# Query tiles between the units of one attention, expert steps in three phases in the other, and unread products in TensorE's waits

## The chip, the cores and the metric

The kernel runs on one core of one Trainium2 chip. The metric is device time in microseconds (us) of one execution; the median of three is used. The engines are TensorE (PE, with its weight loads PEld), VectorE (DVE), ScalarE (ACT), GpSimd (POOL) and SyncE (SP). They run side by side, each through its own list of instructions in order, and meet at semaphores.

## What is computed

One step of a two-layer encoder on 576 tokens of width 1024 (512 of a prompt, 64 of a running stream). Layer 0 mixes tokens with a chunked gMLP; then shared keys and values are made; layer 1 mixes tokens with sliding-window attention. Behind each mixer stands a PEER block, in which every token picks 16 of 16,384 one-neuron experts in each of 8 heads:

```python
q = (xb @ w_q).reshape(blk, PEER_HEADS, 2, D_HALF)
sc = jnp.einsum('thpd,hpnd->thpn', q, sub_keys)
...
act = jax.nn.gelu(jnp.einsum('thkd,td->thk', exp_u[idx], xb))
w = gate * act
return jnp.einsum('thk,thkd->td', w, exp_v[idx])
```

Attention: 16 heads of 64, 4 key heads, a window of three chunks of 64, a bias by distance, and a sink column in the softmax.

## The kernel before

The tokens are split. The "d" (dense) group is 256 of the prompt's tokens (chunks c = 0 and 1, of 128), the "g" (gathered) group is the other 320 (c = 2, 3 and 4, the last of 64). In a PEER block, the d tokens meet all experts: for each of 64 expert pairs TensorE computes `expert_scores` (tile U), ScalarE takes the gelu, VectorE multiplies by a gate matrix (`build`, `one_hot`, `gate_product`), and TensorE adds `expert_sums` (tile V). The g tokens have their chosen experts fetched by indirect DMA: 320 steps a layer, and each step fetches one row of u and v for 128 tokens (128 x 2048 numbers of 4 bytes, 1.05 MB) into one of six slots of gata and gatb. On VectorE a step is a dot product (`dot_x`, L1865) and a weighted add to acc (`axpy`, L1873); between the two ScalarE makes the weight (`weight`, L1243 and L1245: a gelu and a scaling). Those of acc follow each other.

Some of the 320 steps are done early, at named places of other stages. The table `AT` lists the places and how many steps stand at each, `EARLY` is their sum (57 in layer 0, 62 in layer 1), and `step0` spreads the rest over the 64 pairs: 4.5 for each of the first 48, and what is left over the last 16. So a step that is added to `AT` leaves the last 16 pairs of its layer.

The order on every engine is written by hand. A dense product for g tokens is a "tile" of 24 matmuls (L569 to L571: weights and inputs split into a high and a low part, made by ScalarE and GpSimd), and one for d tokens a tile of 8 (L585, 16 rows in the trace). PSUM has eight banks; `plan` counts for each bank how often it is filled (semaphores `full`) and released (`free`), and a product waits until the bank's last reader has released it.

Attention of a group walks over units (j, c), j one of 8 pairs of heads, c one of the group's chunks: 24 units in the g group, 16 in the d group. TensorE's loop runs, for iteration n, the scores of unit n (L937), the transposes of its probabilities three units late (`att_turn`, L954, `LAG` = 3) and the output product four units late (`att_out`, L979). VectorE adds the bias and takes the maximum (`att_max`, L1985 and L1991) and the reciprocal (`att_norm`, L1998); ScalarE does the exponentials (L1363) and copies the transposes to pT (`att_copy`) and the output out of its bank (`att_evac`). In the g group the bank of an output is released by VectorE (`att_low`, L2008), five units late, behind `att_max` and `att_norm` of its iteration. `out_place` names the bank: two in turn for g, one for d. For d tokens the query tiles stand between the units (`Q_AT`); for g tokens all eight stand ahead.

## Time and profile before

| | us |
|---|---|
| median of three executions | 3116.64 (3114.83 to 3118.16) |
| the profiled execution | 3122.2 |
| its span on the core | 3120.4 |

| engine | busy, us | share of the span |
|---|---|---|
| TensorE | 2931.9 | 94% |
| VectorE | 2438.8 | 78% |
| GpSimd | 1011.7 | 32% |
| ScalarE | 797.7 | 26% |

DMA moved 1042.99 MB at a mean of 334 GB/s. The busy share is an average over stages whose limits differ; the rows further down show single stages. The granted clock is 1.00 where TensorE runs at 2.4 GHz and 0.50 where it runs at 1.2 GHz.

### The profile page before, as it was taken

Reading aid. Unit: us, or ns where it says so; the run is one execution under the profiler, and the core shown is the slowest. Engines: PE = TensorE matmul, PEld = TensorE weight load, DVE = VectorE, ACT = ScalarE, POOL = GpSimd, SP = SyncE. Lnnn points to the kernel's source line nnn. Section 1 sums busy time; section 2 is a strip of 40 time slices with the busy share of each in tenths; the row PEclk is TensorE's granted clock in tenths of the full one; section 3 lists DMA queues with packets and bytes.
Section 4 is the critical chain, followed back from the end, with each engine's and each line's share of the span. In section 5 each row is a group of like instructions: output and inputs, shape, how many; then the busy total and the mean of one; then the engine's idle time right before and its main releaser. Section 6 shows DMA issues by size and latency. Waiting matters only on the chain. (4 is left out here: it accounts for less than half of the span.)

```text
span 3120.4 us, 46622 instructions
## 1 busy us (share of the span) xinstructions
PE 2931.9 (94%) x17374; PEld 2572.0 (82%) x17374; DVE 2438.8 (78%) x5309; ACT 797.7 (26%) x2330; POOL 1011.7 (32%) x837
## 2 busy tenths in 40 slices
PE   8899899999999999987898979989999999999977
PEld 7898789888888888876768857879888888888865
DVE  3387899888888888877444777998888888888877
ACT  5432222212211212211453262222212112111212
POOL 5532222322333332333554311222323333333331
PEclk9999999999999999998859989989999999999999
DMA  5327789999999999999403358778999999999996
GB/s 185 116 97 293 305 327 357 398 421 422 421 422 419 420 411 420 414 418 417 150 28 107 121 211 318 275 289 312 419 422 421 422 422 420 415 420 414 413 421 267
DMA packets 159966, 1042.99 MB, mean 334 GB/s; under 512 B 18480, under 2 KB 23920, under 8 KB 44096
## 3 DMA queue, kind: packets, MB, share of 16 engines
q0 software_dynamic: 92160, 671.13, 52.6%
q1 hardware_dynamic: 64224, 357.99, 29.3%
q10 hardware_dynamic: 3424, 11.96, 1.0%
q8 instruction: 75, 1.23, 0.2%
q14 instruction: 83, 0.68, 0.1%
HBM read 1033.28 MB, written 7.86 MB: 334 GB/s over the span
## 5 line engine op out<-in xcount | busy, mean ns | idle before, releaser
L822 PE MATMUL bank<-a,V 128*128 128x256 f32 x4096 | 931.7, 387 | 56.0 <-DVE a L1856 37.6
L809 PE MATMUL bank<-xd,U 128*128 128x256 f32 x4096 | 937.6, 388 | 2.6 <-DMA U<-uvd 2.6
L822 PEld LDWEIGHTS bank<-a,V 128*128 128x128 f32 x4096 | 794.6, 195 | 176.4 <-issue 41.1
L1472 POOL DMA_INDIRECT gata<-uvg,idxg x428 | 511.9, 1196 | 1184.8 <-DVE acc L1873 1148.9
L809 PEld LDWEIGHTS bank<-xd,U 128*128 128x128 f32 x4096 | 788.3, 195 | 110.6 <-DMA U<-uvd 3.6
L1865 DVE CUSTOM_DVE_ANT_0 gata<-gata,xrow 128x1024 f32<-128x1024 f32 x428 | 522.1, 1220 | 229.7 <-DMA gata<-uvg,idxg 225.2
L1243 ACT ACTIVATE act<-dot 128x1 f32<-128x1 f32 x640 | 129.5, 202 | 1669.9 <-DVE dot L1865 1668.0
L1873 DVE SCALAR_TENSOR_TENSOR acc<-gata,wgt,acc 128x1024 f32<-128x1024 f32 x428 | 547.5, 1279 | 5.8 <-ACT wgt L1245 5.6
L1472 POOL DMA_INDIRECT gatb<-uvg,idxg x212 | 235.3, 1110 | 599.0 <-DVE acc L1873 589.2
L1865 DVE CUSTOM_DVE_ANT_0 gatb<-gatb,xrow 128x1024 f32<-128x1024 f32 x212 | 258.8, 1221 | 103.5 <-DMA gatb<-uvg,idxg 101.4
L796 PEld LDWEIGHTS bank<-B,oneA 128*128 128x128 f16 x4096 | 279.1, 150 | 29.4 <-issue 14.1
L796 PE MATMUL bank<-B,oneA 128*128 128x32 f16 x4096 | 283.3, 246 | 13.2 <-DVE B L1845 6.5
L1873 DVE SCALAR_TENSOR_TENSOR acc<-gatb,wgt,acc 128x1024 f32<-128x1024 f32 x212 | 271.3, 1280 | 1.3 <-ACT wgt L1245 1.3
L585 PE MATMUL bank<-xd,raw 128*128 128x256 f32 x896 | 214.6, 396 | 7.2 <-DVE xd L1574 7.2
L585 PEld LDWEIGHTS bank<-xd,raw 128*128 128x128 f32 x896 | 174.9, 199 | 34.0 <-issue 9.4
L569 PE MATMUL bank<-xh,wh 128*128 128x320 f32 x544 | 179.1, 329 | 21.1 <-POOL xl L455 19.5
L1245 ACT ACTIVATE wgt<-act,gateg 128x1 f32<-128x1 f32 x640 | 188.8, 295 | 20.8
L570 PE MATMUL bank<-xl,wh 128*128 128x320 f32 x544 | 170.9, 314 | 0.0
L571 PE MATMUL bank<-xh,wl 128*128 128x320 f32 x544 | 170.8, 314 | 0.0
L1839 DVE TENSOR_TENSOR oneA<-iotaA,i 128x1024 f16<-128x1024 f16 x256 | 170.3, 704 | 0.0
L1507 POOL TENSOR_TENSOR wl<-raw,wh 128x1024 fp32r<-128x1024 f32 x48 | 115.4, 2406 | 106.8 <-ACT wh L1043 106.7
L569 PEld LDWEIGHTS bank<-xh,wh 128*128 128x128 f32 x544 | 105.0, 193 | 30.6 <-issue 29.1
(210 smaller groups left out, 2586.3 us busy)
## 6 DMA issues: line engine op xcount, KB each, us to landing
U<-uvd SPq DMA_DIRECT2D x128, 1024.0 KB
V<-uvd SPq DMA_DIRECT2D x128, 1024.0 KB
raw<-lin SPq DMA_DIRECT2D x152, 512.0 KB
gata<-uvg,idxg POOLq DMA_INDIRECT x428
hsp<-h ACTq DMA_DIRECT2D x2, 2304.0 KB, 16.8
hx<-hsp SPq DMA_DIRECT2D x2, 2304.0 KB, 17.4
gatb<-uvg,idxg POOLq DMA_INDIRECT x212
sk_g<-skT ACTq DMA_DIRECT2D x2, 1024.0 KB, 4.8
```

The lines of the kernel that those rows point to most:

```text
L569: pe.matmul(out, whi, xhi[:, k, :], start=(k == 0), stop=False, skip_group_check=True)
L570: pe.matmul(out, whi, xlo[:, k, :], start=False, stop=False, skip_group_check=True)
L571: mm = pe.matmul(out, wlo, xhi[:, k, :], start=False, stop=(k == DT - 1), skip_group_check=True)
L585: mm = pe.matmul(bank[b][:, 0:TD], raw[:, s, P * k:P * k + P], xo[k][:, :] if name == "od" else x[:, k, :], start=(k == 0), stop=(k == DT ...
L796: mm = pe.matmul(bank[2 + s][:, CHUNK * t:CHUNK * (t + 1)], oneA[:, s, t // TG, :, t % TG], B[:, s, part, :, t], start=(t == 0 and part == ...
L809: mm = pe.matmul(bank[s][:, TD * t:TD * t + TD], U[:, s, o:o + P], xd[:, k, :], start=(t == 0 and k == 0), stop=(k == DT - 1), skip_group_ ...
L822: mm = pe.matmul(bank[b][:, TD * (d % 2):TD * (d % 2) + TD], V[:, s, o:o + P], a[:, s, TD * k:TD * k + TD], start=(first and k == 0 and d ...
L1245: act.activation(wgt[:, k:k + 1], act8[:, k:k + 1], ACT.Copy, scale=gateg[:, s:s + 1])\
L1472: pool.indirect_dma_start(row(l, s), None, uvg[l], bass.IndirectOffsetOnAxis(idxg[:, s:s + 1], 0)).then_inc(g_in[s % SLOTS], 16)
L1839: ins = dve.tensor_tensor(oneA[:, s, u], iotaA[:, :, :], i1[:, None, t + TG * u:t + TG * u + TG].broadcast_to([P, P, TG]), ALU.is_equal)
L1865: dve.tensor_tensor_reduce(u, u, xrow[:, min(s // P, 2), :], 1.0, 0.0, ALU.mult, ALU.add, dot[:, s % 8:s % 8 + 1]).then_inc(dot_done, 1)
L1873: dve.scalar_tensor_tensor(out=acc[:, n, :], in0=row(l, s)[:, D:RD], scalar=wgt[:, s % 8:s % 8 + 1], in1=acc[:, n, :], op0=ALU.mult, op1=A ...
```

## The change

Seven things are done together.

1. In the g attention only two of the eight query tiles stay ahead; the other six (24 matmuls each) stand between the units, in iterations 2, 5, ... 17, and write bank 5. The outputs, which used banks 4 and 5 in turn, all use bank 4. ScalarE's and GpSimd's work on the weights of these tiles, and of the first four of the next product, moves in between too.
2. In the d attention a group of three steps no longer stands in one iteration. The dots stand in iteration n (n = 2, 6, 10, 14), the weights in n + 1, two of the sums in n + 2, the third ahead of the next group's dots.
3. Three more steps stand behind the d attention (`"end"`) and one more in layer 0 (`"two"`).
4. The search of the best experts of chunk 3 in layer 1 (`find_best`) moves from behind the d attention to ahead of it.
5. One of the two query tiles ahead of the d attention moves ahead of `second_rank(1, 0)`.
6. In layer 0 the second chunk's exponential, `second_rank` and `gathered_index` stand one tile earlier.
7. `unused` multiplies a tile of ones by itself, and nothing reads the product: 8 and 20 times at the start, 20 behind `gmlp_g`, 24 at the end of layer 0's experts, 20 behind the g attention's output product.

```diff
 SLOTS = 6
+ATT_DOTS = (2, 6, 10, 14)
...
 AT = (
-    [("mid1", 3), ("two", 1), *[(f"add{m}", 1 + (m in (0, 2, 4))) for m in range(7)], ("mid2", 4),
+    [("mid1", 3), ("two", 2), *[(f"add{m}", 1 + (m in (0, 2, 4))) for m in range(7)], ("mid2", 4),
...
      ("sel3", 3), ("sel4", 3), *[(f"hot{m}", 1 + (m % 4 == 0 or m in (6, 10, 14))) for m in range(LEAD)]],
-    [*[(f"att{n}", 3) for n in (3, 7, 11, 16)], *[(f"add{m}", 1) for m in range(7)], ("mid1", 4),
+    [*[(f"att{n}", 3) for n in ATT_DOTS], ("end", 3), *[(f"add{m}", 1) for m in range(7)], ("mid1", 4),
...
     lin("kvg")
-    lin("qg")
+    seg("qg", b2=1, b3=1)
     seg("vng", b6=2, b7=1)
-    seg("attg", **{f"b{b}": 12 for b in range(8)})
+    seg("qxg", b5=6)
+    seg("attg", b0=12, b1=12, b2=12, b3=12, b4=24, b6=12, b7=12)
...
     seg("qd", b2=1, b3=1)
-    seg("qx", b5=6)
+    seg("qxd", b5=6)
...
-        Q_AT = {2 * m - 3: m for m in range(2, DT)}
+        Q_AT = {"g": {3 * m - 4: m for m in range(2, DT)}, "d": {2 * m - 3: m for m in range(2, DT)}}
...
-            return (4 + n % 2, n // 2) if grp == "g" else (4, n)
+            return 4, n
...
                 xhi, xlo = (oh, ol) if name == "outg" else (xh2, xl2) if name == "qg" else (xh, xl)
-                out = bank[s][:, 0:TG_]
+                b, n = tile_bank(name, m)
+                out = bank[b][:, 0:TG_]
                 pe.wait_ge(lo_done[s], LO[name] + m // 4 + 1)
-                pe.wait_ge(free[s], BASE[name][s] + m // 4)
+                pe.wait_ge(free[b], n)
...
                         norm_sum("n1d", m - 1)
+                    if m == 8:
+                        second_rank(0, 1)
                     if m == 9:
-                        second_rank(0, 1)
-                    if m == 10:
...
                     norm_sums("n5d")
+                else:
+                    pe.wait_ge(free[2], BASE["bld0"][2] + NBLD // 2)
+                    unused(2, 24)
...
+            def unused(b, n):
...
+                for _ in range(n):
+                    pe.matmul(bank[b][:, 0:P], ones[:, :], ones[:, :], start=True, stop=True, skip_group_check=True)
...
                 pe.nop().then_inc(full[b], 1)
+            pe.wait_ge(ones_done, 1)
+            unused(5, 8)
             pe.wait_ge(consts_in, 16 * 2)
-            pe.wait_ge(ones_done, 1)
             norm_sums("n0g")
+            unused(5, 20)
             gmlp_g()
+            unused(5, 20)
...
                 tile("kvg", m, "kv")
-            for m in range(DT):
+            for m in range(2):
...
                         wk = keys(c)[1][m]
-                        mm = pe.matmul(bank[ob][64 * e:64 * e + 64, 0:w], vv, pT[0:wk, n % 2, 2 * e + m, 0:w],
+                        mm = pe.matmul(bank[ob][64 * e:64 * e + 64, 0:w], vv, pT[0:wk, 2 * e + m, 0:w],
...
-                for m in range(DT - 4, DT) if grp == "g" else range(2):
-                    pe.wait_ge(*tile_out(f"q{grp}", m))
+                name, per = f"q{grp}", len(CHUNKS[grp])
+                for m in range(2):
+                    pe.wait_ge(*tile_out(name, m))
...
                     if n < len(UNITS[grp]):
-                        if grp == "d" and n % 2 == 0:
-                            pe.wait_ge(*tile_out("qd", n // 2))
+                        if n % per == 0:
+                            pe.wait_ge(*tile_out(name, n // per))
...
                         att_out(grp, n - LAG - 1)
-                    if grp == "d" and n in Q_AT:
-                        tile_d("qd", Q_AT[n], xd)
-                for n in range(len(UNITS[grp]) - 2, len(UNITS[grp])):
-                    ob, on = out_place(grp, n)
-                    pe.wait_ge(free[ob], BASE[f"att{grp}"][ob] + on + 1)
+                    if n in Q_AT[grp]:
+                        tile(name, Q_AT[grp][n], None, xd)
+                pe.wait_ge(free[4], BASE[f"att{grp}"][4] + len(UNITS[grp]))
...
             added("og", "n4g", None, None, None)
+            unused(5, 20)
...
                 tile_d("kvd", m, xkv, (nv_done, DT * APPLY["kvd"]))
+            tile_d("qd", 0, xd, (nv_done, DT * APPLY["mix1d"]))
...
             gathered_index(1, 0, (1,))
-            for m in range(2):
-                tile_d("qd", m, xd, (nv_done, DT * APPLY["mix1d"]))
+            tile_d("qd", 1, xd)
...
                         gate_exp(0, 0)
-                    if m == 8:
+                    if m == 7:
...
                     if grp == "d":
-                        weights_at(1, f"att{n}")
-                        if n in Q_AT:
-                            query("d", Q_AT[n])
+                        weights_at(1, f"att{n - 1}")
+                    if n in Q_AT[grp]:
+                        query(grp, Q_AT[grp][n])
+                        if grp == "g":
+                            ahead("qg", Q_AT[grp][n])
+                if grp == "d":
+                    weights_at(1, "end")
...
                         low_part(pool, PARTS["mix1"], dt, xl_done)
-            later_lows("qg")
-            first_lows("og")
+            later_lows("qg", (4, 5))
...
                                        ALU.mult).then_inc(pn_done, 1)
+                m = Q_AT["g"].get(n, 0)
+                if 2 <= m < 4:
+                    later_lows("qg", (m + 4,))
+                elif m >= 4:
+                    first_lows("og", (m - 4,))
...
+                return take_best(l, i, find_best(l, i, step))
...
+            def find_best(l, i, step):
...
                 last.then_inc(top_step, 1)
-                step += 1
+                return step + 1
...
+            def take_best(l, i, step):
...
+                c = ORDER[i]
+                n = TCS[c]
...
                 dve.wait_ge(oh_done, n + 1)
-                dve.tensor_tensor(xl[:, j, span("g", c)], bank[4 + n % 2][:, 0:TCS[c]],
-                                  xh[:, j, span("g", c)].bitcast(F32), ALU.subtract).then_inc(free[4 + n % 2], 1)
+                b = out_place("g", n)[0]
+                dve.tensor_tensor(xl[:, j, span("g", c)], bank[b][:, 0:TCS[c]],
+                                  xh[:, j, span("g", c)].bitcast(F32), ALU.subtract).then_inc(free[b], 1)
...
                     if grp == "d":
-                        steps_at(1, f"att{n}")
+                        dots_at(n)
+                        sums_at(n - 2)
+                if grp == "d":
+                    steps_at(1, "end")
...
+            def dots_at(n):
...
+                for k, s in enumerate(early(1, f"att{n}")):
+                    if k == 0 and s > 0:
+                        axpy(1, s - 1)
+                    dot_x(1, s)
...
+            def sums_at(n):
...
+                for s in early(1, f"att{n}")[:-1]:
+                    if s == 0:
+                        dve.wait_ge(acc_zero, 2)
+                    axpy(1, s)
...
             step = choose(1, 0, step)
+            step = find_best(1, 1, step)
...
             normed("n4d", G_FFN1, "d")
-            step = choose(1, 1, step)
+            step = take_best(1, 1, step)
```

TensorE, gathered attention, before: the output product of a unit of chunk 3 in bank 4, then the next iteration, whose output (chunk 4) is in bank 5, then the scores of the next.

```order
L979 MATMUL bank4<-pT_g_113,vnat_118 64x128 x4
L937 MATMUL bank1<-kvs_117,qT_g_108 128x128
L937 MATMUL bank7<-kvs_117,qT_g_108 128x128
L954 MATMUL bank2<-ident_77,S_g_110 128x128 x2
L979 MATMUL bank5<-pT_g_113,cvs_116 64x64
L979 MATMUL bank5<-pT_g_113,vnat_118 64x64
L979 MATMUL bank5<-pT_g_113,cvs_116 64x64
L979 MATMUL bank5<-pT_g_113,vnat_118 64x64
L937 MATMUL bank0<-kvs_117,qT_g_108 128x256
L937 MATMUL bank6<-kvs_117,qT_g_108 128x256
L954 MATMUL bank3<-ident_77,S_g_110 128x128 x4
L979 MATMUL bank4<-pT_g_113,vnat_118 64x128 x2
```

TensorE, the same place in the changed kernel: the transposes of a unit of chunk 4, the output product of chunk 3, and the first rows of a query tile (24 in all).

```order
L969 MATMUL bank2<-ident_77,S_g_110 128x64
L969 MATMUL bank2<-ident_77,S_g_110 64x64
L969 MATMUL bank2<-ident_77,S_g_110 128x64
L969 MATMUL bank2<-ident_77,S_g_110 64x64
L994 MATMUL bank4<-pT_g1_114,vnat_120 64x128 x4
L573 MATMUL bank5<-xh2_60,wh_55 128x320
L574 MATMUL bank5<-xl2_61,wh_55 128x320
L575 MATMUL bank5<-xh2_60,wl_56 128x320
```

The tile now stands between the output and the next scores, in bank 5, and every output product names bank 4.

VectorE, dense attention, before: the iteration that holds the first group of three steps (ISA is the dot product and its read-out).

```order
L1991 TENSOR_REDUCE nm<-S_d_112 128x2
L1998 RECIPROCAL rin<-den 128x2
L2002 TENSOR_SCALAR S_d_111<-S_d_111,rin 128x256
L1865 ISA gata,dot<-gata,xrow 128x1024
L1865 ISA dot 128x1
L1865 ISA gata,dot<-gata,xrow 128x1024
L1865 ISA dot 128x1
L1873 SCALAR_TENSOR_TENSOR acc<-gata,wgt,acc 128x1024
L1865 ISA gata,dot<-gata,xrow 128x1024
L1865 ISA dot 128x1
L1873 SCALAR_TENSOR_TENSOR acc<-gata,wgt,acc 128x1024
L1979 COPY S_d_111<-snk 128x2
```

VectorE, dense attention, in the changed kernel: the iteration with the first three dots, and the start of the next.

```order
L2023 TENSOR_REDUCE nm<-S_d_111 128x2
L2030 RECIPROCAL rin<-den 128x2
L2034 TENSOR_SCALAR S_d_112<-S_d_112,rin 128x256
L1897 ISA gata,dot<-gata,xrow 128x1024
L1897 ISA dot 128x1
L1897 ISA gata,dot<-gata,xrow 128x1024
L1897 ISA dot 128x1
L1897 ISA gata,dot<-gata,xrow 128x1024
L1897 ISA dot 128x1
L2011 COPY S_d_112<-snk 128x2
L2017 SCALAR_TENSOR_TENSOR S_d_112<-dst,bank 128x256 x2
L2023 TENSOR_REDUCE nm<-S_d_112 128x2
```

And its next iteration but one, with two of the sums.

```order
L2011 COPY S_d_111<-snk 128x2
L2017 SCALAR_TENSOR_TENSOR S_d_111<-dst,bank 128x256 x2
L2023 TENSOR_REDUCE nm<-S_d_111 128x2
L2030 RECIPROCAL rin<-den 128x2
L2034 TENSOR_SCALAR S_d_112<-S_d_112,rin 128x256
L1905 SCALAR_TENSOR_TENSOR acc<-gata,wgt,acc 128x1024 x2
L2011 COPY S_d_112<-snk 128x2
```

The dots and the sums, which alternated in one iteration, now stand two iterations apart.

## Rows read from the trace of the kernel before

**Rows 1.** The page's 40 slices: the DMA share in tenths.

```profile
DMA  5327789999999999999403358778999999999996
```

**Rows 2.** The page's groups: one line of expert products.

```profile
L809 PE MATMUL bank<-xd,U 128*128 128x256 f32 x4096 | 937.6, 388 | 2.6 <-DMA U<-uvd 2.6
```

**Rows 3.** Busy time by stretch, with TensorE's granted clock and DMA share.

```profile
core 0: us, PE busy (x) PEld busy (x) DVE busy (x) ACT busy (x) POOL busy (x), PEclk, DMA share, GB/s
135.30:140.60 5.30, 5.08 (x24) 4.86 (x25) 4.05 (x8) 2.16 (x5) 2.83 (x3) 0.73 0.30 94
1521.60:1565.20 43.60, 43.49 (x290) 42.54 (x291) 14.87 (x21) 20.48 (x36) 33.42 (x18) 1.00 0.40 132
1566.50:1638.60 72.10, 65.93 (x368) 42.48 (x369) 37.99 (x145) 38.30 (x154) 38.81 (x49) 0.54 0.06 17
1766.80:1775.10 8.30, 7.10 (x33) 5.90 (x32) 8.23 (x74) 2.05 (x3) 6.47 (x13) 1.00 0.41 132
1790.90:1875.60 84.70, 60.76 (x384) 44.43 (x385) 57.62 (x130) 50.46 (x149) 15.19 (x11) 0.84 0.58 225
3000.00:3074.00 74.00, 58.85 (x248) 49.21 (x246) 52.69 (x68) 9.96 (x40) 23.66 (x19) 0.94 1.01 419
```

**Rows 4.** Timeline, TensorE: one triple of the gathered attention; then one row of the dense.

```profile
1599.75 1.22 PE L937 MATMUL bank<-kvs,qT_g 64*128 64x256 f32 x4
1601.95 0.70 PE L979 MATMUL bank<-pT_g,vnat 128*64 128x128 f32 x4
1602.58 0.70 PE L937 MATMUL bank<-ck,qT_g 64*64 64x128 f32 x4
1604.20 1.13 PE L979 MATMUL bank<-pT_g,vnat 128*64 128x128 f32 x8
1605.26 0.80 PE L937 MATMUL bank<-kvs,qT_g 64*128 64x128 f32 x4
1606.60 0.48 PE L979 MATMUL bank<-pT_g,cvs 128*64 128x64 f32 x2
...
1608.22 0.80 PE L937 MATMUL bank<-kvs,qT_g 64*128 64x256 f32 x2
...
1818.50 0.72 PE L937 MATMUL bank<-kvs,qT_d 64*128 64x128 f32 x8
```

**Rows 5.** Timeline, VectorE, in the same two places.

```profile
1601.01 0.75 DVE L1985 SCALAR_TENSOR_TENSOR S_g<-dst,bank 128x256 f32<-128x256 f32 x2 [2.07 <-PE bank L937]
1602.53 0.20 DVE L2008 TENSOR_TENSOR xl<-bank,xh 128x64 fp32r<-128x64 f32 x1
1604.76 0.26 DVE L2008 TENSOR_TENSOR xl<-bank,xh 128x128 fp32r<-128x128 f32 x1
1607.07 0.26 DVE L2008 TENSOR_TENSOR xl<-bank,xh 128x128 fp32r<-128x128 f32 x1
...
1819.24 0.75 DVE L1985 SCALAR_TENSOR_TENSOR S_d<-dst,bank 128x256 f32<-128x256 f32 x2 [7.82 <-PE bank L937]
```

**Rows 6.** Who waited, TensorE, dense attention (1790.9 to 1875.6).

```profile
PE bank L979 <- ACT xo L1399: 23.5, 8, 7.3
```

**Rows 7.** Groups of lines, VectorE, dense attention.

```profile
L1873 DVE SCALAR_TENSOR_TENSOR acc<-gata,wgt,acc 128x1024 f32<-128x1024 f32 x8 | 10.3, 1282 | 1.9 <-ACT wgt L1245 1.9
L1865 DVE CUSTOM_DVE_ANT_0 gata<-gata,xrow 128x1024 f32<-128x1024 f32 x8 | 9.7, 1218 | 0.0
```

**Rows 8.** Timeline, ScalarE, one table load in the dense attention.

```profile
1801.91 1.28 ACT L1243 ACT_TABLE_LOAD   x1
```

**Rows 9.** Who waited: TensorE at 127 to 142.

```profile
PE bank L569 <- POOL xl L455: 6.3, 1, 6.3
```

**Rows 10.** Who waited: TensorE at 255 to 275.

```profile
PE bank L627 <- ACT vn_d L1089: 1.4, 1, 1.4
```

**Rows 11.** Who waited: VectorE at 1783 to 1792.

```profile
DVE S_d L1985 <- PE bank L937: 8.1, 1, 8.1
```

**Rows 12.** Who waited: TensorE at 1774 to 1778.

```profile
PE bank L744 <- issue: 3.1, 1, 3.1
```

More of the change, by code:

```diff
@@ L254, in program @@
               "d1": at_("S_d1", 155712, [P, 2, 2, 2 * P + 1], F32)}
-        pT_ = {"g": at_("pT_g", 36928, [P, 2, 4, P], F32), "d": at_("pT_d", 87040, [P, 2, 4, P], F32)}
+        pT_ = {"g": [at_(f"pT_g{s}", 36928 + 2048 * s, [P, 4, P], F32) for s in range(2)],
+               "d": [at_(f"pT_d{s}", o, [P, 4, P], F32) for s, o in enumerate((153600, 209504))]}
         ck = at_("ck", 41024, [P, 2, P], F32)
@@ L403, in tile_bank @@
         def tile_bank(name, m):
-            if name != "qd":
+            if name not in ("qg", "qd"):
                 return m % 4, BASE[name][m % 4] + m // 4
             if m < 2:
-                return 2 + m, BASE["qd"][2 + m]
-            return 5, BASE["qx"][5] + m - 2
+                return 2 + m, BASE[name][2 + m]
+            return 5, BASE["qx" + name[1]][5] + m - 2
         def tile_done(name, m):
@@ L573, in tile_g @@
                         mid()
-                mm.then_inc(full[s], 1)
+                mm.then_inc(full[b], 1)
             def tile_d(name, m, x, ready=None, mid=None):
@@ L960, in att_out @@
                 j, c = UNITS[grp][n]
-                w, pT = TCS[c], pT_[grp]
+                w, pT = TCS[c], pT_[grp][n % 2]
                 base = BASE[f"att{grp}"]
@@ L1345, in query @@
                                scale=DH ** -0.5).then_inc(free[b], 1)
-            for m in range(DT):
+            for m in range(2):
                 query("g", m)
@@ L1375, in att_copy @@
                 j, c = UNITS[grp][n]
-                w, wks, pT = TCS[c], keys(c)[1], pT_[grp]
+                w, wks, pT = TCS[c], keys(c)[1], pT_[grp][n % 2]
                 base = BASE[f"att{grp}"]
@@ L1382, in att_copy @@
                 if wks == [P, P]:
-                    act.activation(pT[:, n % 2, :, :], bank[2 + n % 2][:, :].rearrange("p (a q) -> p a q", a=4),
+                    act.activation(pT[:, :, :], bank[2 + n % 2][:, :].rearrange("p (a q) -> p a q", a=4),
                                    ACT.Copy).then_inc(free[2 + n % 2], 1)
@@ L1386, in att_copy @@
                 src = bank[2 + n % 2][:, :].rearrange("p (e m q) -> p e m q", e=2, m=2)
-                dstp = pT[:, n % 2, :, :].rearrange("p (e m) q -> p e m q", e=2)
+                dstp = pT[:, :, :].rearrange("p (e m) q -> p e m q", e=2)
                 for m, wk in enumerate(wks):
@@ L1500, in first_lows, with later_lows @@
                                        ALU.subtract).then_inc(lo_done[m], 1)
-            def later_lows(name):
-                for m in range(4, count(name)):
+            def later_lows(name, tiles=None):
+                for m in tiles or range(4, count(name)):
                     s = m % 4
```

## The prediction

> **What bounds the kernel now.** I read the page's slices first: the DMA share is near full from slice 7 to 19 and from 29 on, and low between, where layer 1 starts [rows 1]. So the expert phases run at the pace of their bytes (3000 to 3074: DMA 1.01 at 419 GB/s [rows 3]), and the rest at the pace of TensorE or of a chain through it. The busy time by stretch then shows three kinds of stretch outside the expert phases [rows 3]. Twelve tiles of the g kind take 43.6 us, full, at clock 1.00: 3.6 us a tile. The gathered attention takes 72.1 us with TensorE busy for 65.9, but at clock 0.54: the engine is full and slow. The dense attention takes 84.7 us with TensorE busy for 60.8 at clock 0.84, and its waits are one line: 23.5 us in 8 waits for ScalarE's copy of an output [rows 6]. A change outside the expert phases moves the end by what it saves there; one inside them counts by its bytes.
>
> **The change, part by part.** The sum is made against the profiled execution's own 3122.2 us, which lies 5.6 above the median of the runs; the difference is then taken from the median.
>
> *Four steps done earlier.* A step fetches 1.05 MB, and leaves the last 16 pairs of its layer, where DMA is full: 1.05 MB at 419 GB/s is 2.5 us [rows 3]. Four give -10.0. Where they go, VectorE has room: a step costs it a dot and a sum, 2.5 us [rows 7], and the stretch behind the dense attention has TensorE alone at work. Bounds: -10 (all bytes count), 0 (something else sets the tail's pace, for there TensorE is busy 58.9 of 74 us).
>
> *The gathered attention.* The stage and its six tiles now cost 72.1 + 6 x 3.6 = 93.7 us. Take one triple of units, from the scores of chunk 3 at 1599.75 to the next at 1608.22: 8.47 us, TensorE never waiting [rows 4]. With one bank, the output product in an iteration must wait until `att_low` of the same iteration has released it, and that stands on VectorE behind the maximum, which waits for this iteration's scores. The rows give how long that is, from the start of the scores to the end of L2008: 1602.73 - 1599.75 = 2.98, 1605.02 - 1602.58 = 2.44, 1607.33 - 1605.26 = 2.07 [rows 4, 5]. Behind each comes the output product, 0.63, 1.06 and 1.62 by the starts of the rows [rows 4]. With 0.1 a piece for the hand-over (an estimate) the triple is 11.1 us at 1.2 GHz. At 2.4 GHz the scores reach VectorE after 0.74 instead of 1.26 [rows 4, 5]; I take 0.52, 0.35 and 0.30 off the three and 0.59 (0.74/1.26) of the outputs: 6.3 + 2.0 + 0.3 = 8.6. So the second bank's loss costs what the clock can give back. Six triples carry a tile: 12.2 at 2.4 GHz; at 1.2 GHz 11.1 + 7.2 = 18.3. The first triple has no outputs to wait for, -2.7. All at 2.4: 6 x 12.2 + 2 x 8.6 - 2.7 = 87.7, or -6. All at 1.2: 129, or +36. Which? Before, the clock fell in the attention, where the matmuls are narrow, and came back with tiles; the dense attention, which has tiles between its units and waits too, was granted 0.84, that is a third of its time at 1.2 GHz [rows 3]. With the same third here, about a quarter of the work is at 1.2: 6 x 13.7 + 2 x 9.2 - 2.7 = 98. I take 97, **+3**, for the tiles take a little less of the cycle than there. GpSimd's weight parts hide behind the tile, and nobody on the chain waits for them.
>
> *The dense attention.* Before, a group's three dots and sums take VectorE about 7.3 us (3 x 1.15 + 3 x 1.2 and a short wait [rows 7]), and ScalarE's table load of 1.28 [rows 8], weights and second load lie beside them. In the changed order VectorE's block is 3 dots and a sum, 4.7 us, and ScalarE's block (two table loads, three weights, a query copy: 4.3 us) comes behind the next exponential, which waits for the maximum behind the dots. So the two no longer lie side by side: 9.0 instead of 7.3, +1.7 a group, and the two sums later hold the maximum up for 2.4, which TensorE's tile covers in part. Over four groups I take +8. The last group, formerly in the drain, is in the loop and cannot hide behind a tile. Against it: the query tile that moved ahead of `second_rank` fills a wait of 3.1 us [rows 12]. Net **+5**; bounds -15 (the phases hide the blocks, and most of the 23.5 goes) and +10.
>
> *`find_best`* takes 8.2 us of VectorE (the stretch 1766.8 to 1775.1, which is the same work on chunk 2 [rows 3]), and lands where VectorE waits 8.1 us for the first scores [rows 11]: 0. Where it left, VectorE gets no earlier, for its next product waits for TensorE's `second_rank`, whose place behind the third tile is the same: 0. Without that cover it would cost 8.
>
> *Layer 0's chunk one tile earlier*: VectorE reaches the copy that TensorE waits 1.4 us for sooner [rows 10]: **-1.4**, bounds 0 and -3. The extra step there fits in VectorE's slack.
>
> *The unread products.* One costs half of a 128 x 256 product, which is two records of 0.229 us [rows 2]: 0.23, and 20 cost 4.6 us. They stand in two waits of 6.3 us, behind `gmlp_g` [rows 9] and behind the g output product, where the kernel's wait is of the same kind, so they delay nothing. What they can give is the next tile's start: 5.3 us at clock 0.73 instead of 3.6 [rows 3], so 1.7 a place, 3.4 in all. I take three quarters, **-2.6**, since a wait of some 2 us is left. The Trainium skill (TensorE: Matmul & The Clock Gate, Part 1) says that the slow clock is the default and that activity lifts it; by that both places give their 1.7, and the sum would be 0.8 lower. At the start and at the end of layer 0's experts the wait left behind them is several us long: 0. Bounds -5 and, if they run at 1.2 GHz and outlast the wait (9.2 us against 6.3), +6.
>
> Sum: -10.0 + 3 + 5 - 1.4 - 2.6 = -6.0. From 3122.2 that is 3116.2 for such a profiled execution, and from the median 3116.6 it is **3110.6**. What a measurement of this kernel can tell from no change is about 0.2%, 6.2 us, so the forecast lies on the edge between "same" and "faster".
>
> **The rivals.**
>
> *The clock holds.* If the tiles keep 2.4 GHz through the gathered attention, the stage is 87.7 and the sum -15: **3102**. For it: tiles brought the clock back each time, and between two of them are only 8.6 us. Against it: the same narrow products ran at 0.54 with TensorE full.
>
> *The clock falls between the tiles* (the slower side). The waits for bank 4 leave TensorE idle for about 1.3 us in each unit, more than a third of the time between tiles, on top of narrow products. If each tile starts at 1.2 GHz and the attention behind it falls back soon, six tenths of the work is at 1.2: 6 x 15.9 + 2 x 10.1 - 2.7 = 113, or +19 instead of +3: **3127**. It decides from a stage of about 103 us on (no gain left), and is slower by over 0.2% from 109. The Trainium skill (same page, HAM oscillation) describes bursts between waits that each start cold; by that this rival is the likelier one, and here it would be a tile of over 5 us in each triple.
>
> *The three phases hide the blocks.* If dots, weights and sums each fit behind a unit and a tile, the 23.5 us shrink to 5 and the stage gives -15 to -20: **3090**. For it: a block alone is shorter than before. Against it: ScalarE's block now has no partner.
>
> *The early steps are worth nothing*, since VectorE or TensorE paces the tail: -10 falls away: **3120**. Against it: DMA at 1.01 in the very stretch.
>
> **How the numbers follow.** Forecast as it stands (3104 to 3117): 0.36, half of it over the edge. Clock holds: 0.20. Phases hide: 0.12. Clock falls: 0.18, nearly all slower by over 0.2%. Steps worth nothing: 0.14, a third of it slower in company of a dearer dense attention. Faster by over 0.2%: 0.18 + 0.20 + 0.12 = 0.50; slower: 0.18 + 0.05 = 0.23; same: 0.27. The range leaves out the deeper half of "phases hide" and the dearer part of "clock falls": 3093 to 3127.
>
> **What would show it.** Right: in the gathered attention a wait at the line of the output product for VectorE's line of `att_low` in nearly every unit, of 1 to 1.5 us; a granted clock near 0.85; the stage with its tiles 93 to 100 us. In the dense attention waits for ScalarE's copy of 25 to 35 us. The tile behind `gmlp_g` under 4 us. The last 16 pairs 7.5 us shorter in layer 1 and 2.5 in layer 0. Wrong: no waits for bank 4, or a clock of 0.6 there; a dense attention under 75 us; tails as long as before.

## The result, and the profile after

The changed kernel takes 3134.57 us (median of five, 3133.22 to 3138.15), the kernel before 3117.05 (five, 3114.83 to 3121.56). The ratio is 1.0054 with a 95% interval of 1.0042 to 1.0065: slower by 13 to 20 us, where 3110.6 was forecast with a range of 3093 to 3127. The profiled execution of the changed kernel has a span of 3132.8 against 3120.4, 12.4 us more. That is less than the 17.5 us between the medians, because the profiled execution of the kernel before (3122.2 us) lies 5 us above its median; the forecast's sum was made against that execution too, and gave -6.0 there.

Where the time went is read from TensorE's instructions, the same one in both traces. By how much it comes later than before:

| place | before | changed | later by |
|---|---|---|---|
| first product behind layer 0's experts (a shared-key tile) | 1521.6 | 1520.1 | -1.5 |
| end of the gathered attention's last output | 1638.0 | 1654.2 | 16.2 |
| first scores of the dense attention | 1790.9 | 1804.4 | 13.5 |
| end of its last output | 1875.2 | 1896.9 | 21.7 |
| first sums of pair 48, layer 1 | 2942.4 | 2962.2 | 19.7 |
| end of the last sums | 3095.0 | 3107.2 | 12.2 |

So the gathered attention and its tiles lost 17.7 us, the dense attention 8.2; the stretch between them gained 2.7, the work from there to pair 48 2.0 and the last 16 pairs 7.5. Busy time by stretch (columns as in rows 3), the kernel before: the gathered attention from its first scores to its last output, and the dense attention.

```profile
1567.00:1638.00 71.00, 65.93 (x368) 42.45 (x368) 37.51 (x143) 38.01 (x152) 38.45 (x49) 0.53 0.05 17
1790.90:1875.20 84.30, 60.75 (x384) 44.42 (x384) 57.62 (x130) 50.18 (x148) 15.19 (x11) 0.84 0.58 224
```

The changed kernel: the gathered attention with the six tiles in it, and the dense attention.

```profile
1544.40:1654.20 109.80, 83.60 (x512) 64.21 (x512) 40.47 (x143) 46.95 (x164) 52.30 (x55) 0.71 0.13 40
1804.40:1896.90 92.50, 61.86 (x384) 45.09 (x384) 63.67 (x156) 49.95 (x148) 18.41 (x14) 0.82 0.56 205
```

109.8 us stand against 92.6 of before (71.0 and six tiles of 3.6), at a clock of 0.71. Who waited, TensorE, in the gathered attention (1531 to 1652; the very last output, behind it, waits 0.8 us more):

```profile
PE bank L994 <- DVE xl L2041: 22.9, 21, 2.7
```

This is the wait that the forecast named: the output product for the release of bank 4 by `att_low`, 21 times, 1.1 us on average. In the dense attention the same view has, against 23.5 us in 8 waits [rows 6]:

```profile
PE bank L994 <- ACT xo L1414: 26.0, 11, 5.3
PE bank L994 <- ACT pT_d L1398: 2.5, 1, 2.5
```

And behind `gmlp_g`, where 6.3 us of wait stood [rows 9], the unread products leave:

```profile
PE bank L573 <- POOL xl L458: 1.8, 1, 1.8
```

The timeline of TensorE shows what follows the waits for bank 4: rows of a triple with its tile, then the start of the next tile.

```profile
1573.28 1.13 PE L994 MATMUL bank<-pT_g,vnat 128*64 128x128 f32 x8 [1.06 <-DVE xl L2041]
1574.34 0.64 PE L573 MATMUL bank<-xh,wh 128*128 128x320 f32 x1
1574.77 0.47 PE L574 MATMUL bank<-xl,wh 128*128 128x320 f32 x1
...
1578.23 0.31 PE L575 MATMUL bank<-xh,wl 128*128 128x320 f32 x1
...
1578.91 0.49 PE L952 MATMUL bank<-kvs,qT_g 64*128 64x128 f32 x4
...
1584.43 0.69 PE L994 MATMUL bank<-pT_g,vnat 128*64 128x128 f32 x4 [1.32 <-DVE xl L2041]
...
1587.64 1.13 PE L994 MATMUL bank<-pT_g,vnat 128*64 128x128 f32 x8 [1.06 <-DVE xl L2041]
1588.70 0.64 PE L573 MATMUL bank<-xh,wh 128*128 128x320 f32 x1
```

The tile begins with products of 0.64 and 0.47 us (1.2 GHz) and ends with products of 0.31 (2.4 GHz), so it takes 4.6 us; the six tiles take 3.78 (the first, at 2.4 GHz throughout), 5.23, 4.64, 5.86, 5.03 and 6.07. The clock comes back within each of the five others, holds for the narrow products behind it (scores in 0.49), and is down again when the next tile begins (the output ahead of it: 1.13).

### The profile page after: what moved, and what is told of

The parts are those of the page before. It is cut to its first block and busy times, and to the rows that moved or that the text cites. A ratio compares the mean times of both kernels' runs of the same rounds, so it can differ in the third digit from the quotient of the medians.

```text
span 3132.8 us, 46992 instructions
## 1 busy us (share of the span) xinstructions
PE 2942.9 (94%) x17558; PEld 2586.7 (83%) x17558; DVE 2443.1 (78%) x5309; ACT 798.2 (25%) x2330; POOL 1032.8 (33%) x837
## 5 line engine op out<-in xcount | busy, mean ns | idle before, releaser
L1491 POOL DMA_INDIRECT gatb<-uvg,idxg x212 | 257.2, 1213 | 522.3 <-DVE acc L1905 513.4
L573 PEld LDWEIGHTS bank<-xh,wh 128*128 128x128 f32 x544 | 107.0, 197 | 20.4 <-issue 16.6
```

Source lines behind the costliest of these rows:

```text
L573: pe.matmul(out, whi, xhi[:, k, :], start=(k == 0), stop=False, skip_group_check=True)
L1491: pool.indirect_dma_start(row(l, s), None, uvg[l], bass.IndirectOffsetOnAxis(idxg[:, s:s + 1], 0)).then_inc(g_in[s % SLOTS], 16)
```

## The experiments

"Theory" and "rival" in a quoted text are the outcomes named before the run. Every kernel was timed against the kernel before on the same chip, in four lots (the first four rows, the next four, four, three), in which the kernel before took 3117.9, 3118.5, 3120.5 and 3117.1. Across lots the ratios are the safer measure.

| kernel | time | ratio to before | 95% interval |
|---|---|---|---|
| e_gback | 3110.6 | 0.9977 | 0.9968 to 0.9986 |
| e_turnsg | 3111.9 | 0.9982 | 0.9973 to 0.9991 |
| e_nounused | 3133.1 | 1.0048 | 1.0034 to 1.0062 |
| e_onebank | 3135.9 | 1.0053 | 1.0039 to 1.0066 |
| e_steps | 3109.7 | 0.9966 | 0.9956 to 0.9977 |
| e_three | 3130.1 | 1.0033 | 1.0020 to 1.0046 |
| e_gdback | 3107.8 | 0.9967 | 0.9954 to 0.9980 |
| e_turnsgd | 3113.6 | 0.9986 | 0.9977 to 0.9996 |
| e_gfill | 3118.0 | 0.9995 | 0.9986 to 1.0004 |
| e_fill28 | 3136.1 | 1.0052 | 1.0038 to 1.0066 |
| e_nofind | 3104.7 | 0.9946 | 0.9932 to 0.9960 |
| e_best | 3109.2 | 0.9966 | 0.9954 to 0.9978 |
| e_bfill | 3112.6 | 0.9983 | 0.9974 to 0.9992 |
| e_turnsfill | 3097.2 | 0.9937 | 0.9923 to 0.9950 |
| e_backnofindfill | 3099.3 | 0.9946 | 0.9933 to 0.9960 |

### The gathered attention: one bank

**e_gback**: the changed kernel, its gathered attention as before.

```diff
-    seg("qg", b2=1, b3=1)
+    lin("qg")
...
-        Q_AT = {"g": {3 * m - 4: m for m in range(2, DT)}, "d": {2 * m - 3: m for m in range(2, DT)}}
+        Q_AT = {"g": {}, "d": {2 * m - 3: m for m in range(2, DT)}}
...
-            return 4, n
+            return (4 + n % 2, n // 2) if grp == "g" else (4, n)
...
```

> The changed kernel with the gathered attention as it was before (all eight query tiles ahead, outputs in banks 4 and 5 in turn), everything else of the change kept. Theory 1 (the 15 us that TensorE's instructions are late by the end of the gathered attention belong to this part, and nothing later gives them back): 3134.6 - 15 = 3119.6. Rival (a part of them is taken up later by a wait that is there anyway): 3125 or more.

Measured: 3110.6, 24 us below the changed kernel, and 9 below what theory 1 gave. Its sense held, its size did not: in the two traces the last output lies 18.6 us apart, the last sums 25. So nothing of it is given back, and some 6 us more appear behind it, 3.6 of them in the last 16 pairs.

**e_onebank**: the kernel before, one bank for the outputs and nothing else.

```diff
-            return (4 + n % 2, n // 2) if grp == "g" else (4, n)
+            return 4, n
...
```

(The release in `att_low` and the banks' counts follow it.)

> The kernel before, with all outputs of the gathered attention in bank 4 (tiles still ahead, nothing else changed). Theory 1 (the chain scores, maximum, release, output is the cost, 11.1 us instead of 8.5 a triple at 1.2 GHz, seven triples): +18, 3135. Rival (VectorE releases a bank early enough, only some units wait): +8, 3125.

Measured: 3135.9, +18, where theory 1 had 3135. Busy time of the stage, and under it who waited:

```profile
1567.50:1657.20 89.70, 66.89 (x368) 42.72 (x368) 37.48 (x143) 39.05 (x152) 38.56 (x49) 0.53 0.04 13
```

```profile
PE bank L979 <- DVE xl L2008: 18.5, 22, 1.1
```

The stage is 89.7 instead of 71.0 at the same clock and the same busy time, and the whole difference of 18.7 is this wait. Tiles and attention together are 135.1 us here and 134.1 in the changed kernel: with one bank, putting tiles between the units brought 1 us.

**e_turnsg**: the changed kernel, outputs and tiles in banks 4 and 5 in turn.

```diff
+            if grp in TURNS:
+                k = USES[grp].index(("o", n))
+                return 4 + k % 2, k // 2
             return 4, n
...
+            if name[1] in TURNS:
+                k = USES[name[1]].index(("q", m))
+                return 4 + k % 2, BASE["att" + name[1]][4 + k % 2] + k // 2
             return 5, BASE["qx" + name[1]][5] + m - 2
...
```

(`USES` lists outputs and tiles in their order; `TURNS` is "g".)

> The changed kernel, but the outputs and the query tiles of the gathered attention take banks 4 and 5 in turn (output, output, output, tile, ...), so that an output waits for the last but one release. Theory 1 (the waits for bank 4, 22.9 us in 21, cost their own time, and without them the tiles are granted 2.4 GHz from their start more often): the stage loses 22 us of waits and some 8 us of slow tiles, -25 to -30: about 3107. Rival (the narrow products alone bring the clock down; then scores, transposes and outputs run longer at 1.2 GHz and eat half of it): 3122.

Measured: 3111.9, 22.7 below the changed kernel, nearer to theory 1. Busy time of the stage, and who waited in it:

```profile
1545.90:1635.30 89.40, 72.73 (x512) 56.22 (x512) 40.70 (x143) 45.30 (x164) 52.03 (x55) 0.85 0.16 49
```

```profile
PE bank L1003 <- ACT pT_g L1408: 7.2, 6, 1.4
PE bank L1003 <- DVE xl L2051: 5.3, 5, 1.1
```

Of 22.9 us of waits for the release 5.3 are left, 7.2 have gone over to ScalarE's copy of the transposes. The clock is 0.85: tiles of 3.8 us and of 5.3 to 5.6 alternate. But it is no faster than e_gback with tiles ahead (3110.6).

### The gathered attention: the clock

**e_gfill**: the changed kernel, 19 of its output products with four unread products ahead of each (20 in the text below, but the loop reaches 19: the stage has 152 matmul rows more, 8 a place).

```diff
                     if 0 <= n - LAG - 1:
+                        if grp == "g" and n + 1 < len(UNITS[grp]):
+                            pe.wait_ge(free[(n + 1) % 2], BASE["attg"][(n + 1) % 2] + (n + 1) // 2)
+                            unused((n + 1) % 2, 4)
                         att_out(grp, n - LAG - 1)
```

> The changed kernel with four more unread products ahead of every output product of the gathered attention but the last four (into the bank of the next scores; nothing waits for them but TensorE itself), 20 places. It tells the waits for bank 4 from the clock that follows them. Theory 1 (the waits bring the clock down, and the tiles then start at 1.2 GHz: 5.0 to 6.1 us instead of 3.7): filled waits keep 2.4 GHz, a triple is 12.5 us instead of 14.8, the stage 12 us shorter, 3121. Rival (the clock falls in the narrow products all the same; at 1.2 GHz four products are 1.9 us in a wait of 1.1): 0.8 us more in 20 places, 3148.

Measured: 3118.0, 16.6 below the changed kernel. Busy time of the stage, who waited in it, and TensorE's timeline from one tile to the next:

```profile
1544.90:1639.50 94.60, 83.80 (x664) 68.98 (x664) 40.25 (x143) 46.32 (x164) 52.30 (x55) 0.96 0.15 46
```

```profile
PE bank L994 <- DVE xl L2044: 9.4, 22, 1.8
```

```profile
1574.32 0.42 PE L573 MATMUL bank<-xh,wh 128*128 128x320 f32 x1
...
1578.73 1.06 PE L898 MATMUL bank<-ones 128*128 128x128 f32 x8
1579.95 0.30 PE L994 MATMUL bank<-pT_g,cvs 128*64 128x64 f32 x2 [0.16 <-DVE xl L2044]
...
1586.74 0.41 PE L573 MATMUL bank<-xh,wh 128*128 128x320 f32 x1
```

The clock is 0.96 instead of 0.71, a triple 12.42 us from tile to tile (14.9 on average in the changed kernel, from 1559.38 to 1618.95 for four), and five of the six tiles take 3.8 (the first takes 6.1). The outputs still wait for the one bank, now with work in the wait. By the ratios it is 18 us. So holding the clock gives back 16.6 to 18 of the 24 us that this part costs, and e_turnsg, which takes the waits away, gives back 22.7. These are not two shares of one sum: with the clock held the scores come sooner and the waits for the bank are shorter too, and part of the gain comes without any bank wait, as the next run shows.

**e_bfill**: the kernel before, with the same unread products (same edit, 19 places).

> The kernel before (tiles ahead, two banks) with four unread products ahead of each of 20 output products of the gathered attention. Theory 1 (full-width products among the narrow ones hold 2.4 GHz): the stage's 66 us of products take 33 to 36, the unread ones 19, the chain through ScalarE some waits more: about 60 instead of 71 us, 3109. Rival (the clock falls all the same): the unread products are 1.85 us in 20 places, 3157.

Measured: 3112.6, 4.6 below before. The stage:

```profile
1569.80:1636.90 67.10, 62.18 (x520) 48.03 (x520) 37.48 (x143) 38.13 (x152) 38.40 (x49) 0.89 0.05 18
```

It is 67.1 instead of 71.0 us, at 0.89 instead of 0.53. Here TensorE hardly waited before (5.1 us of the 71, in 5 waits), so the clock falls with the attention's own narrow products alone, and wide ones among them hold it. I had expected 60: the unread products take 19 times 0.9 us themselves, and the mean clock is 0.89, not 1.00.

### The dense attention

**e_three**: the kernel before, its twelve steps in three phases and nothing else.

```diff
-    [*[(f"att{n}", 3) for n in (3, 7, 11, 16)], *[(f"add{m}", 1) for m in range(7)], ("mid1", 4),
+    [*[(f"att{n}", 3) for n in (2, 6, 10, 14)], *[(f"add{m}", 1) for m in range(7)], ("mid1", 4),
...
-                        weights_at(1, f"att{n}")
+                        weights_at(1, f"att{n - 1}")
...
-                        steps_at(1, f"att{n}")
+                        dots_at(n)
+                        sums_at(n - 2)
...
```

> The kernel before with nothing but the three phases of the dense attention (dots in iterations 2, 6, 10 and 14, weights one later, sums two later; the same twelve steps). Theory 1 (ScalarE's block of table loads, weights and query copy and VectorE's block no longer lie side by side): the stage is 8 us longer, as in the trace of the changed kernel, so 3125. Rival (the stage is longer only because other parts of the change stand in it: the query tile and the search ahead of it): 3118 to 3120.

Measured: 3130.1, +11.6. The stage went from 84.3 to 91.0 us:

```profile
1793.60:1884.60 91.00, 62.67 (x384) 45.65 (x384) 58.24 (x130) 49.96 (x148) 15.55 (x11) 0.80 0.57 208
```

Who waited, TensorE:

```profile
PE bank L979 <- ACT xo L1399: 25.0, 11, 5.3
PE bank L979 <- ACT pT_d L1383: 3.3, 1, 3.3
```

Against 23.5 us in 8 waits [rows 6]: the longest wait is shorter (5.3 against 7.3), but there are twelve of them instead of eight, for four groups: three stops of the chain a group instead of two.

**e_turnsgd**: e_turnsg with the banks in turn in the dense attention too (`TURNS = "gd"`).

> The changed kernel with outputs and query tiles in banks 4 and 5 in turn in both attentions. Theory 1 (in the dense attention most of the 26 us of waits are for ScalarE's blocks, which also hold up its copy of the transposes; a second bank frees only the short waits of 1.05 and 1.47 us in 6 places): -6 to -8 against the same change in the gathered attention alone, 3105. Rival (the output bank is the whole wait): -20, 3092. Rival (nothing: every wait just moves to the copy of the transposes): 3112.

Measured: 3113.6, no better than e_turnsg. Who waited:

```profile
PE bank L1002 <- ACT pT_d L1407: 21.8, 7, 5.3
PE bank L1002 <- ACT xo L1423: 2.6, 2, 1.3
```

The last expectation held: of 28.5 us of waits 24.4 are left, and the wait for the output bank has become one for the copy of the transposes. It is ScalarE's order that stops the chain, not the bank.

**e_gdback**: the changed kernel with both attentions as before (`ATT_DOTS = (3, 7, 11, 16)` and `steps_at`, besides e_gback's edit).

> The changed kernel with both attentions as they were before; left of the change are the four early steps, the search and the query tile ahead of the dense attention, layer 0's rank one tile earlier and the unread products. Theory 1: the 3110.6 of the changed kernel with the gathered attention alone put back, less the 8 us of the three phases: 3103. Rival (a shorter dense attention only makes the experts wait for DMA, which has not got further): 3108 or more.

Measured: 3107.8, 2.8 below e_gback and not the 8 of theory 1. The next run shows what the search has to do with it.

**e_nofind**: e_gdback with the search of chunk 3 back behind the dense attention.

```diff
             step = choose(1, 0, step)
-            step = find_best(1, 1, step)
             attention("d")
...
-            step = take_best(1, 1, step)
+            step = choose(1, 1, step)
```

> The changed kernel with both attentions as before (3107.8) and, besides, the search of the best experts of chunk 3 where it was, behind the dense attention. Theory 1 (my prediction: the search hides ahead of the attention and frees nothing behind it): 3107.8, no difference. Rival (its 8 us of VectorE ahead of the attention delay the first bias and maximum, of which the trace shows 1.9 and 0.4 us of waits): 3105. Rival (it frees the selection behind): 3111.

Measured: 3104.7, the ratio lower by 0.0021, with intervals that overlap. What decides is the trace. Busy time of the dense attention in e_gdback and who waited at its start, then the same stretch in e_nofind:

```profile
1785.30:1873.00 87.70, 62.82 (x384) 46.07 (x384) 64.17 (x170) 50.26 (x148) 18.82 (x15) 0.85 0.59 223
```

```profile
PE bank L951 <- DVE S_d L2019: 2.3, 2, 1.9
PE bank L968 <- ACT S_d L1387: 1.6, 1, 1.6
```

```profile
1784.90:1868.00 83.10, 58.47 (x384) 43.09 (x384) 60.45 (x134) 50.26 (x148) 17.39 (x14) 0.87 0.60 228
```

The search makes the first maximum late (VectorE's first bias starts 6.1 us after the first scores in e_gdback, 0.75 in e_nofind), TensorE waits 3.9 us in the first iterations, and the next query tile runs at 1.2 GHz (6.09 us instead of 3.62). Without it the stage is 4.6 us shorter. With the three phases as well it is 91.6 (e_gback) or 92.5 (the changed kernel): the two losses, 6.7 and 4.6 apart, are 7.3 to 8.2 together, which is why putting back the phases alone gave so little.

### Steps and unread products

**e_steps**: the kernel before with the four early steps.

```diff
-    [("mid1", 3), ("two", 1), *[(f"add{m}", 1 + (m in (0, 2, 4))) for m in range(7)], ("mid2", 4),
+    [("mid1", 3), ("two", 2), *[(f"add{m}", 1 + (m in (0, 2, 4))) for m in range(7)], ("mid2", 4),
...
-    [*[(f"att{n}", 3) for n in (3, 7, 11, 16)], *[(f"add{m}", 1) for m in range(7)], ("mid1", 4),
+    [*[(f"att{n}", 3) for n in (3, 7, 11, 16)], ("end", 3), *[(f"add{m}", 1) for m in range(7)], ("mid1", 4),
...
```

> The kernel before with nothing but the four steps done earlier (one more at 'two' in layer 0, three at 'end' behind the dense attention, whose own steps stay in iterations 3, 7, 11 and 16). Theory 1 (each step is 1.05 MB less in a tail that runs at 419 GB/s): -10, 3107.5. Rival (only layer 1's count, since layer 0's tail came out only 1 us shorter in the changed kernel): -8 to -9, 3109. Rival (steps are worth nothing, something else paces the tail): 3117.5.

Measured: 3109.7, -8.8, or -10.6 by the ratio. So the steps are worth about what was forecast. That the gain lies in the last 16 pairs the traces do not show: of 8.9 us between the two profiled executions, 3.7 lie in layer 1's last 16 pairs (148.9 against 152.6 us) and 5.2 ahead of them, and in e_onebank, where no step moved, the same pairs are 4.3 shorter (148.3).

**e_nounused**: the changed kernel, the five places of `unused` empty.

> The changed kernel without its unread products (all five places). Theory 1 (the traces show the instructions behind each place neither earlier nor later than before): 3134.6, within 1.5 us. Rival (my prediction's term: 2.6 us are gained by them): 3137.

Measured: 3133.1. Nothing is lost without them.

**e_fill28**: 29 instead of 20 of them behind the gMLP and behind the gathered output product.

> The changed kernel with 29 instead of 20 unread products behind the gMLP and behind the gathered attention's output product, so that they reach to the end of the wait (1.8 us of 6.3 is left open by 20). Theory 1 (any rest of a wait is enough to start the next tile at 1.2 GHz; without a rest it starts at 2.4): the two tiles behind take 3.6 instead of 5.3 us each, -3, 3131. Rival (the products of 128 columns do not hold the clock, whatever the rest): 3134, the tiles as long as now.

Measured: 3136.1, no gain. The same stretch behind the gMLP by busy time, in e_nounused and in e_fill28 (where the tile starts later, at 136.5, behind the last of the unread products):

```profile
135.30:141.60 6.30, 5.87 (x30) 5.75 (x31) 4.46 (x9) 2.93 (x8) 3.19 (x4) 0.69 0.34 120
```

```profile
135.30:141.60 6.30, 5.40 (x36) 4.59 (x35) 5.25 (x11) 3.37 (x8) 3.79 (x4) 1.00 0.25 73
```

With 29 no wait stays, and the tile runs at 2.4 GHz. With 20 of them 1.8 us stay open, and the outcome differs by place. The changed kernel behind the gMLP, then behind the gathered output product:

```profile
129.05 4.63 PE L898 MATMUL bank<-ones 128*128 128x128 f32 x40
135.52 0.38 PE L573 MATMUL bank<-xh,wh 128*128 128x320 f32 x1 [1.84 <-POOL xl L458]
135.74 0.38 PE L574 MATMUL bank<-xl,wh 128*128 128x320 f32 x1
135.91 0.47 PE L575 MATMUL bank<-xh,wl 128*128 128x320 f32 x1
...
1689.24 4.63 PE L898 MATMUL bank<-ones 128*128 128x128 f32 x40
1695.70 0.38 PE L573 MATMUL bank<-xh,wh 128*128 128x320 f32 x1 [1.83 <-POOL xl L458]
1695.92 0.31 PE L574 MATMUL bank<-xl,wh 128*128 128x320 f32 x1
```

In the first the clock falls after two products, in the second the whole tile runs at 2.4 GHz. Over the ten kernels with 20 of them, 8 of the 20 tiles behind such a rest are at 2.4 GHz throughout, in 11 the clock falls after 2 to 9 of the 24 products, and one begins at 1.2; without unread products all twelve (six kernels) begin at 1.2.

What it is worth in time is another matter. Behind the gMLP, counted from the end of the norm sums, its last product ends after 11.78 us in the kernel before, in the changed one and without unread products, and after 11.77 with 29. In e_fill28's timeline the tile now waits inside:

```profile
140.44 0.38 PE L573 MATMUL bank<-xh,wh 128*128 128x320 f32 x1 [0.84 <-DVE xl L458]
```

The tile goes at the pace at which VectorE and GpSimd make the low parts of its input: at neither place, in any trace, does it end before 11.77 us. Where the clock falls in the middle of it it ends later, by up to 0.6 us with 20 unread products ahead.

### Put together

**e_best**: e_turnsg with the dense attention's steps back in iterations 3, 7, 11 and 16.

> The version to which the runs point: the changed kernel with two banks in turn for outputs and tiles of the gathered attention, and the dense attention's steps back in iterations 3, 7, 11 and 16. Theory 1 (parts add up: 3111.9 with two banks in turn, less the 3 to 8 us of the three phases): 3106. Rival (the tiles between the units gain 2 us over tiles ahead, as the stage's 113.7 against 115.7 shows): 3105. Rival (noise: same as with both attentions put back): 3108.

Measured: 3109.2, and the ratio is that of e_gdback. The rival of "the same" held.

**e_turnsfill**: e_best, the search back behind the dense attention, and e_gfill's unread products.

> The changed kernel with two banks in turn, four unread products ahead of 20 outputs, the dense attention's steps where they were and the search of chunk 3 where it was. Theory 1 (clock held, triples of about 12.2 us, as long as now): the unread products give nothing over two banks in turn, 3105. Rival (the tiles' 5.3 us fall to 3.8 and the unread ones hide in the waits): 3099. Rival (they delay the chain): 3110.

**e_backnofindfill**: e_nofind with e_gfill's unread products.

> The changed kernel with both attentions and the search as before (3104.7), and four unread products ahead of 20 outputs of the gathered attention. Theory 1 (the gain of the kernel before with them adds up, -9): 3096. Rival (they cost in this arrangement what they give): 3105.

Measured: 3097.2 and 3099.3, both faster than the kernel before and the changed one; between them the intervals overlap. The unread products' own share in e_backnofindfill is open: its ratio, 0.9946, is that of e_nofind without them, so the 9 us of theory 1 did not come, though the stage is 3.5 us shorter (67.1 against 70.6), as in e_bfill:

```profile
1565.60:1636.20 70.60, 65.49 (x368) 42.13 (x368) 37.50 (x143) 38.01 (x153) 38.44 (x49) 0.54 0.05 17
1566.70:1633.80 67.10, 61.56 (x520) 47.69 (x520) 37.48 (x143) 38.12 (x152) 38.42 (x49) 0.91 0.05 18
```

Against e_best, e_turnsfill changes two things, the products and the search, and no run parts them in the total. Of e_turnsfill: busy time of the stage, its wait for the release, and the first products of two tiles, two triples apart:

```profile
1545.70:1631.50 85.80, 80.91 (x664) 66.57 (x664) 40.57 (x143) 45.91 (x164) 52.44 (x55) 0.98 0.16 51
```

```profile
PE bank L1003 <- DVE xl L2054: 0.8, 5, 0.2
```

```profile
1571.35 0.41 PE L582 MATMUL bank<-xh,wh 128*128 128x320 f32 x1
...
1594.67 0.41 PE L582 MATMUL bank<-xh,wh 128*128 128x320 f32 x1
```

Triples of 11.66 us, at a clock of 0.98, hardly a wait: 85.8 us for what took 92.6 before and 109.8 in the changed kernel.

## Why the prediction was wrong

**The step that failed** is "with the same third here, about a quarter of the work is at 1.2". I took the clock's share from the dense attention, and expected a clock near 0.85. It was 0.71: nearly six tenths of the stage's time at 1.2 GHz, and by the triple (14.9 us, between 12.2 and 18.3) about 44% of its work. So the term of +3 came out as +17.2. The terms on both sides of it were right: the wait of about 1.1 us in nearly every unit, the price of the one bank at the low clock (e_onebank, +18 us, its waits 18.5 of the 18.7 that the stage grew), the triple at 2.4 GHz (12.2 worked out, 12.4 measured once the clock was held, with the unread products in its waits), and the rival "the clock falls between the tiles" (15.9 us a triple and +19; 14.9 and +17.2 for the stage). That rival came true, and held the sign: with its +19 the sum is +10, where the two traces are 12.4 apart and the medians 17.5. The Trainium skill (TensorE: Matmul & The Clock Gate, A second HAM failure mode: psum-queue depth-cycling) tells of this pattern, short idles between groups of matmuls and a cost paid between them; the trace agrees, with five of six tiles at 4.6 to 6.1 us instead of 3.8. What I had quoted, HAM oscillation on the same page of the Trainium skill, is a case of waits that are longer than the work between them; the waits here are 1.1 us, and still the tiles start cold. I had given the rival 0.18. What I should have seen in the rows of before: the narrow products had brought the clock to 0.54 without a wait, so with waits added nothing spoke for two thirds of the time at full speed.

**Early steps**, -10.0: right in size, -8.8 measured alone (-10.6 by the ratio). In the changed kernel the last 16 pairs are 7.5 us shorter in layer 1 and 2.4 in layer 0 (from 159.5 to 157.1), nearly the numbers forecast (7.5 and 2.5), but that is in part luck: with the same steps and nothing else (e_steps) they are 3.7 and 1.6 shorter.

**Dense attention**, +5: the net is +4 (e_gback's trace is 2.3 us ahead of before at the scores of the selection and 1.5 behind at the attention's end), but made of other pieces. The three phases cost 6.7 in the stage (8 forecast) and 11.6 in the time of the kernel alone (9.6 in its trace, 2.9 of them in layer 0, which it leaves alone). The search was put at 0; its place costs 4.6 in the stage and 3 to 6 in the time, with intervals that overlap. I had set its 8.2 us against a wait of 8.1 [rows 11]. But the query tile that moved ahead of `second_rank` brings the first scores nearer to the end of VectorE's selection, to 5.9 us in the changed kernel and 4.2 in e_gdback from 7.7 before, so the cover shrank in the same change; and the search took 10.0 and 10.4 us there, not 8.2, with waits between its steps (2.2 us of them in e_gdback). The moved tile's own gain came, 3.5 us.

**Layer 0**, -1.4: the first expert product is 2.1 us earlier in the changed kernel, but it is 0.9 earlier in e_three too, which leaves layer 0 alone; too small to tell. Of that and the 2.4 of the tail only 1.5 are left at the end of layer 0: the 48 pairs between took 3.6 us more, as they did in e_three.

**Unread products**, -2.6: nothing. The clock rose where they stand, in part of the traces for the whole tile, but the tile ends no sooner, for its inputs come no faster. The sign that I had named, a tile behind `gmlp_g` of under 4 us, stayed out: it takes 5.5, as before.

**What stays open**: between e_gback and the changed kernel 18.6 us lie at the end of the gathered attention and 25 at the end. The last 16 pairs take 141.4 us in the one and 145.0 in the other with the same steps. No run takes this apart, and with one trace a kernel the differences of a few us in the expert phases may be no more than those between executions. Open is also what the unread products are worth in a kernel whose tiles stand ahead: 5.3 us by the ratio in e_bfill, nothing by the ratio in e_backnofindfill.

## What to carry to other kernels

When two buffers are made one to make room for something, follow the chain from the release back through the reader's own queue: here it went through this iteration's scores, and the bank was worth 18 us. Price the clock for the stage as it will be: here narrow products and waits of 1 us together kept TensorE at 1.2 GHz for nearly six tenths of the time, and a wide tile every 15 us did not hold the clock. And a cover belongs to a change as a whole: behind what one part moves forward, another can no longer hide.

## What the runs showed of the hardware

Unread products hold the granted clock among narrow ones (0.53 to 0.89 in the kernel before, 0.71 to 0.96 in the changed one). They gave 4.6 us in the one and 16.6 in the other, where the stage hangs on TensorE's own products, and nothing behind the two waits of 6.3 us, where the tile waits for its inputs. Behind 4.6 us of them and a rest of 1.8 us, 8 of 20 tiles ran at 2.4 GHz throughout, and in 11 the clock fell after 2 to 9 products; without them all twelve began at 1.2. And 22 waits of 0.8 us cost exactly their sum (18.5 of 18.7 us) where the clock was down already.
